# One operation for scale and modulation in the norms, query tokens first, modulation chunks moved, retention's gain folded into its gate

## What is computed

```python
def first_block(...):                      # DEPTH = 2
    for l in range(2):
        # six vectors of 1024 each, from c and from c_ctx: shift, scale, gate (mix), shift, scale, gate (ffn)
        sh_a, sc_a, g_a, sh_f, sc_f, g_f = adaln(c, mod_w[l], mod_b[l])
        csh_a, ... = adaln(c_ctx, mod_w[l], mod_b[l])
        hx = modulate(rms_norm(x, norm_mix_g[l]), sh_a, sc_a)      # n(x) * (1 + scale) + shift
        hc = modulate(rms_norm(ctx, norm_mix_g[l]), csh_a, csc_a)
        y_x, y_c = even_mixer(...) if l == 0 else odd_mixer(...)   # odd: queries from hx alone, keys and values from both
        x = x + g_a * (y_x @ w_out[l])
        x = x + g_f * swiglu(modulate(rms_norm(x, norm_ffn_g[l]), sh_f, sc_f), ...)
        # the same for ctx in layer 0

def second_block(...):                     # DEPTH = 2
    ...
    hr = retention_chunkwise(...)                                   # 4 heads of 512
    y_r = silu(rg) * (normalized(hr) * r_norm_g[i])                 # gate, norm, weight
    merged = sigmoid(gm) * (y_m @ w_bm[i]) + sigmoid(gr) * (y_r @ w_br[i])
    ...
    x = x + sigmoid(h3 @ w_pe_gate[i]) * (p[i] @ w_pe[i])
    return rmsnorm(x, final_g)
```

## Time and profile before

| | before |
|---|---|
| median of 3 runs | 2436.9 us (2436.57 to 2437.91) |
| profiled execution: time, span | 2438.51 us, 2436.7 us |
| busy: TensorE, VectorE, ScalarE | 95%, 62%, 42% of the span |
| mean granted clock of TensorE | 0.979 of full speed |
| chain that ended last | TensorE 83%, VectorE 9%, ScalarE 3%, waits without a cause in the profile 2%, DMA 2% |
| HBM read | 386 MB, 159 GB/s over the span |

### The profile page before, as it was taken

The page is one execution under the profiler, slowest core; times in us unless marked ns, Lnnn a source line. Parts: engine busy times, 40 slices in busy tenths (PEclk is TensorE's granted clock), DMA queues, the critical chain, the costliest instruction groups (busy, mean ns, idle before and its releaser), DMA issues.

```text
span 2436.7 us, 33036 instructions
## 1 busy us (share of the span) xinstructions
PE 2307.2 (95%) x14198; PEld 1987.7 (82%) x14198; DVE 1513.5 (62%) x1866; ACT 1015.4 (42%) x1223; POOL 0.2 (0%) x4
## 2 busy tenths in 40 slices
PE   6978989999998888999999999999999999999997
PEld 3755667777786767999999877999989988789997
DVE  3877553333347667555678767675668766767475
ACT  4245541111224145434664345443456534444343
POOL 0000000000000000000000000000000000000000
PEclk9989999999998999999999999999999999999999
DMA  8440034444323241455555453555445445344552
GB/s 321 169 176 1 25 139 192 166 188 170 124 104 121 87 104 64 146 189 190 212 199 183 175 186 138 182 177 187 182 182 203 178 177 194 143 173 178 186 183 94
DMA packets 61401, 389.19 MB, mean 160 GB/s; under 512 B 6600, under 2 KB 11080, under 8 KB 16072
## 3 DMA queue, kind: packets, MB, share of 16 engines
q1 hardware_dynamic: 61256, 387.08, 43.6%
HBM read 386.01 MB, written 1.05 MB: 159 GB/s over the span
## 4 chain that ended last, share of the span: by engine, by line
PE 83%; DVE 9%; ACT 3%; issue 2%; DMA 2%; SPq 0%; DVEq 0%; ACTq 0%
PE PS L479 25%; PE PS L480 25%; PE PS L481 25%; DVE w_lo L1565 2%; DMA raw<-chunks_in 1%; PE PS L783 1%; PE PS L929 1%; PE PS L665 1%; ACT w_hi L1135 1%; PE PS L626 1%; DVE stat L1760 1%; PE PS L911 1%; PE PS L690 1%; ACT xn L1213 1%; DVE BIG L1769 1%
## 5 line engine op out<-in xcount | busy, mean ns | idle before, releaser
L1565 DVE TENSOR_TENSOR w_lo<-raw,w_hi 128x2048 fp32r<-128x2048 f32 x300 | 683.5, 2290 | 506.7 <-ACT w_hi L1135 504.9
L1135 ACT ACTIVATE w_hi<-raw 128x2048 fp32r<-128x2048 f32 x300 | 571.7, 1913 | 749.5 <-PE PS L481 448.8
L479 PE MATMUL PS<-x_hi,w_hi 128*128 128x256 f32 (+1 forms) x2048 | 629.4, 307 | 12.2 <-DVE x_lo L1630 7.8
L480 PE MATMUL PS<-x_lo,w_hi 128*128 128x256 f32 (+1 forms) x2048 | 626.9, 306 | 0.0
L481 PE MATMUL PS<-x_hi,w_lo 128*128 128x256 f32 (+1 forms) x2048 | 626.5, 306 | 0.0
L479 PEld LDWEIGHTS PS<-x_hi,w_hi 128*128 128x128 f32 x2048 | 393.9, 192 | 38.0 <-issue 21.1
L480 PEld LDWEIGHTS PS<-x_lo,w_hi 128*128 128x128 f32 x2048 | 394.0, 192 | 16.7
L481 PEld LDWEIGHTS PS<-x_hi,w_lo 128*128 128x128 f32 x2048 | 393.8, 192 | 16.8
L479 PE MATMUL PS<-w_hi,x_hi 128*128 128x512 f32 (+1 forms) x800 | 317.7, 397 | 21.6 <-DVE w_lo L1565 9.8
L480 PE MATMUL PS<-w_lo,x_hi 128*128 128x512 f32 (+1 forms) x800 | 313.6, 392 | 0.0
L481 PE MATMUL PS<-w_hi,x_lo 128*128 128x512 f32 (+1 forms) x800 | 313.2, 391 | 0.0
(11 more groups left out here) (284 smaller groups left out, 2259.5 us busy)
## 6 DMA issues: line engine op xcount, KB each, us to landing
raw<-chunks_in SPq DMA_DIRECT2D x348, 1024.0 KB, 4.8
bias_ring<-brows_in SPq DMA_DIRECT2D x32, 256.0 KB, 5.1
G<-nrows_in SPq DMA_DIRECT2D x2, 1536.0 KB, 6.6
free_b<-rel_in SPq DMA_DIRECT2D x4, 512.0 KB, 8.0
BIG<-rel_in SPq DMA_DIRECT2D x4, 512.0 KB, 9.1
tabt<-tabs_in SPq DMA_DIRECT2D x1, 1536.0 KB, 12.3
X<-x_in SPq DMA_DIRECT2D x1, 1024.0 KB, 8.3
X<-ctx_in SPq DMA_DIRECT2D x1, 1024.0 KB, 10.3
```

The source lines that it names most:

```text
L479: pe.matmul(o, lhs[0], rhs[0], start=start, stop=False, **more)
L480: pe.matmul(o, lhs[0], rhs[1], start=False, stop=False, **more)
L1135: act.activation(w_hi[:, i % HI_RING, :], ring[:, n % RING, :], ACT.Copy).then_inc(*hi_ready.now(n))
L1565: dve.tensor_tensor(w_lo[:, c % RING, :], ring[:, c % RING, :], w_hi[:, i % HI_RING, :].bitcast(F32), ALU.subtract).then_inc(*lo_ready.now(c))
```

## The change

- **Norms.** Outside ("mix", 0) VectorE makes scale and modulation in one operation: X times the modulation's scale times the broadcast root, 256 columns each; ScalarE adds the shift while it rounds to `x_hi`; VectorE's subtraction adds the shift as well. In ("mix", 0) the 8 products with the root come first, each linked to the next by a wait; then the modulation's values, the `w_lo` of the first weight chunk, and then for each tile scale and shift on VectorE from SBUF, with the rounding on ScalarE.
- **Query tokens first.** In ("mix", 1) all 8 tiles of the query tokens come before the 8 of the context tokens, since the first product (`od_q`) takes query tokens alone; the `w_hi` and `w_lo` of its third and fourth chunk go between the context tiles.
- **Modulation chunks.** In `w_out` of layer 0 two mod chunks stand after its first, second and fourth chunk (6 in place of 4). Pack 3 is turned after the third chunk, its copy and its values (`modulation(3)`, `modulation(0, 2)`) move ahead of squares and into the residual. The SwiGLU holds 2 mod chunks fewer; `mod_end(1, 0)` moves to before its last product. `ffn_step` stays as it is. At the start the fifth mod chunk goes between the two halves of `root_of_squares`.
- **`w_lo` out of the residuals.** One `w_lo` each moves from within the residuals of `w_out` and of the last `ffn_out` of layer 0 to behind them.
- **Retention.** The weight is multiplied into the gate `rg` (`gained`, four operations of 2 x 512 columns) while the heads are still computed; its four operations in `norm_r` go.
- **The end.** The table load of the square root stands after the third pair of squares, and VectorE's sums of the third pair after its last addition to X.

```diff
+        def who_order(key, tiles):
+
+            return [(0,), (1,)] if key == ("mix", 1) else [tuple(range(tiles // 2))]
...
-            def root_of_squares(key, tiles, bank=7):
+            def root_of_squares(key, tiles, bank=7, meanwhile=None):
 
                 acc, n = sums[tiles][0], tiles * P
                 pe.wait_ge(*x_summed.after(key, KD - 1))
@@ -591,9 +595,11 @@
                 for t in range(tiles):
                     mm = pe.matmul(PS[:, bank, t:t + 1], acc[:, t * P:(t + 1) * P], tab("ones")[:, 0:1], start=True, stop=True)
                 mm.then_inc(*sums_bc.now(key))
+                if meanwhile:
+                    meanwhile()
                 pe.wait_ge(*rstd_diag.after(key))
                 pe.matmul(PS[:, bank, 0:n], tab("ones"), sums[tiles][2][0], start=True, stop=True).then_inc(*rstd_bc.now(key))
-                reader[bank] = scaled.after(key, KD - 1)
+                reader[bank] = scaled.after(key, tiles // 2 - 1, KD - 1)
...
+            def mod_two():
+
+                mod_chunk()
+                mod_chunk()
...
+                    if l == 0 and last:
+                        mod_end(1, 0)
...
-                    if l == 0 and part == 1:
-                        mod_end(1, 0)
...
-            project_feat("w_out", 0, 2, hT[4], width=512, freed=updated("w_out", 0), need=copied("y0"), between=mod_row)
-            mod_end(0, 2)
+            project_feat("w_out", 0, 2, hT[4], width=512, freed=updated("w_out", 0), need=copied("y0"),
+                         between=at_steps({0: mod_two, 1: mod_two, 2: lambda: mod_end(0, 2), 3: mod_two}))
...
+                for whos in who_order(key, tiles):
+                    for k in range(KD):
+                        act.wait_ge(*scaled.after(key, whos[-1], k))
+                        for w in whos:
+                            cols = slice(w * 256, w * 256 + 256)
+                            if key != ("mix", 0):
+                                ins = act.activation(hT[tiles][0][:, k, cols], full[tiles][:, k, cols], ACT.Identity,
+                                                     bias=modc[l][:, kind * 8 + k, w:w + 1])
+                        if key == ("mix", 0):
+                            ins = act.activation(hT[tiles][0][:, k, :], full[tiles][:, k, :], ACT.Copy)
+                        ins.then_inc(*copied_s.now(key, whos[-1], k))
+                        if middle and k + KD * whos[0] in middle:
+                            middle[k + KD * whos[0]]()
...
             split_to(first + 2)
+            modulation(3)
             for k in range(KD):
                 act.wait_ge(*x_ready.after("w_out", 0, k // 4, k % 4))
                 square(("ffn", 0), 4, k)
                 if k == 3:
                     split_to(first + 3)
                     split_to(first + 4)
-            modulation(3)
...
+            first_od = place_of[plan["first chunk", "od_q", 1]]
+            norm_mod(("mix", 1), 4, 0, {8: lambda: split_to(first_od + 2), 12: lambda: split_to(first_od + 3)})
...
-                    if l and n == 3:
-                        act.activation(stat[:, 20:21], eps, ACT.Sqrt)
                     for m in (n - 1, n) if n % 2 else ():
                         act.wait_ge(*x_ready.after("pe_g", l, m // 2, m % 2))
                         for k in (2 * m, 2 * m + 1):
                             tail(key, k, l == 0)
+                        if l and m == 2:
+                            act.activation(stat[:, 20:21], eps, ACT.Sqrt)
...
+                early = key == ("mix", 0)
+
+                def scale(whos, k):
+                    for w in whos:
+                        cols = slice(w * 256, w * 256 + 256)
+                        o = full[tiles][:, k, cols]
+                        if early:
+                            ins = dve.tensor_scalar(o, o, modc[l][:, kind * 8 + 8 + k, w:w + 1],
+                                                    modc[l][:, kind * 8 + k, w:w + 1], ALU.mult, ALU.add)
+                            continue
+                        ins = dve.scalar_tensor_tensor(full[tiles][:, k, cols], X[:, w, k, :],
+                                                       modc[l][:, kind * 8 + 8 + k, w:w + 1], PS[:, bank, cols], ALU.mult, ALU.mult)
+                    ins.then_inc(*scaled.now(key, whos[-1], k))
+
+                def low(whos, k):
+                    dve.wait_ge(*copied_s.after(key, whos[-1], k))
+                    if early:
+                        hi, lo = (a[:, k, :] for a in hT[tiles])
+                        ins = dve.tensor_tensor(lo, full[tiles][:, k, :], hi.bitcast(F32), ALU.subtract)
+                    for w in () if early else whos:
+                        cols = slice(w * 256, w * 256 + 256)
+                        hi, lo = (a[:, k, cols] for a in hT[tiles])
+                        ins = dve.scalar_tensor_tensor(lo, full[tiles][:, k, cols], modc[l][:, kind * 8 + k, w:w + 1],
+                                                       hi.bitcast(F32), ALU.add, ALU.subtract)
+                    ins.then_inc(*copied_v.now(key, k if whos[-1] == tiles // 2 - 1 else ("x", k)))
+
+                if early:
+                    for k in range(KD):
+                        link(dve.tensor_tensor(full[tiles][:, k, :].rearrange("p (w t) -> p w t", w=2), X[:, :, k, :],
+                                               PS[:, bank, 0:n].rearrange("p (w t) -> p w t", w=2), ALU.mult))
                     modulation(*mod)
-                for k in range(KD):
-                    if k + lead < KD:
-                        scale(k + lead)
-                    low(k)
+                if ahead:
+                    ahead()
+                steps = [(whos, k) for whos in who_order(key, tiles) for k in range(KD)]
+                for step in steps[:lead]:
+                    scale(*step)
+                for i, step in enumerate(steps):
+                    if i + lead < len(steps):
+                        scale(*steps[i + lead])
+                    low(*step)
                     if at_tile:
-                        at_tile(k)
+                        at_tile(i)
...
+                        first_od = place_of[plan["first chunk", "od_q", 1]]
+                        residual("ffn_out", l, 5, 2 * part, key, lambda j, i: lo_to(first_od - 2 + 2 * j) if i == 0 else None)
+                        lo_to(first_od + 1)
...
+            def ahead(j, i):
+                if i == 0:
+                    lo_to(ev + 12 + j)
+                if (j, i) == (1, 0):
+                    modulation(0, 2)
+
+            residual("w_out", 0, 2, 0, ("ffn", 0), ahead)
+            lo_to(ev + 14)
+            norm_mod(("ffn", 0), 4, 2, None, lambda k: lo_to(ev + 15) if k == 5 else None)
             swiglu(0, 4, ("mix", 1))
-            norm_mod(("mix", 1), 4, 2, None, lambda k: lo_for("ffn_out", 0, 5) if k == 3 else None)
+            first_od = place_of[plan["first chunk", "od_q", 1]]
+            norm_mod(("mix", 1), 4, 2, None, lambda i: lo_to(first_od + 2 + (i > 9)) if i in (9, 13) else None)
...
-                    for t in range(2):
-                        ins = dve.tensor_tensor(hr[t][:, cols], hr[t][:, cols], G[:, 1024:3072][:, cols], ALU.mult)
-                    link(ins)
                     for t in range(2):
                         ins = dve.tensor_tensor(hr[t][:, cols], hr[t][:, cols], rg[:, t, cols], ALU.mult)
                     link(ins, y_ready, "yr", l, part)
                     if part == 0:
                         merge_m(l, 0)
                         lo_to(first_bm + 3)
+
+            def gained(l, j):
+
+                dve.wait_ge(*tok_acted.after("rg", l, j, 0))
+                cols = slice(512 * j, 512 * j + 512)
+                gain = G[:, 1024:3072][:, cols].unsqueeze(1).to_broadcast([P, 2, 512])
+                link(dve.tensor_tensor(rg[:, :, cols], rg[:, :, cols], gain, ALU.mult))
...
                         if h == 3:
                             lo_for("gr", l, 1)
+                            gained(l, 2)
                             copy_turned(("ym", l), 0, 4)
                         biased("gr", l, 1, wide(gr), h - 2)
+                    if h < 2:
+                        gained(l, h)
                     if h in (1, 2):
                         r_out(h - 1)
                 r_copy(2)
+                gained(l, 3)
                 copy_turned(("ym", l), 4, 4)
                 head_stats("hr", 2, hr, 512)
...
-                    if n % 2:
+                    if n == 1 or n == 3 and l == 0:
                         finish(key, [k - 2, k - 1], l == 0)
                     dve.wait_ge(*tok_acted.after("pe_g", l, n))
                     link(dve.tensor_tensor(t, t, pw[:, k:k + 2, :], ALU.mult))
                     dve.tensor_tensor(X[:, 0, k:k + 2, :], t, X[:, 0, k:k + 2, :],
                                       ALU.add).then_inc(*x_ready.now("pe_g", l, n // 2, n % 2))
+                    if n == 3 and l:
+                        finish(key, [k - 2, k - 1], False)
```

(6 more changed lines are left out.)

55 lines of the change are left out of this document (13 added, 42 removed).

## The result

| | before | after |
|---|---|---|
| median (7 runs each, side by side) | 2437.22 us | 2445.96 us |
| range | 2436.57 to 2439.76 | 2442.55 to 2447.87 |
| profiled execution: time, span | 2438.51, 2436.7 us | 2447.41, 2445.6 us |
| mean granted clock | 0.979 | 0.975 |

The change makes the kernel slower: ratio 1.0031 (95% interval 1.0022 to 1.0040), some 8.7 us by the medians (7.6 by the ratio) in place of the forecast gain of 6.1. In the code after, the products of a weight chunk are L483 to L485 (L479 to L481 before), mod chunks L789 (L783), turns of modulation rows L768 (L762), turns of activations L632 (L626), `w_hi` L1146, `w_lo` L1574, ScalarE's copy of a pack L1297.

What follows compares the result with a forecast made beforehand. The prediction took TensorE to bound the kernel (83% of the chain). Its terms, +11.6 for new SwiGLU waits less slot 11, then -2.1, -1.4, -6.3, -0.7, -5.2, -2.05, summed to -6.15: median 2430.8 us, range 2423 to 2438.

Steps and rivals of the forecast that it cites:

- The start: First product of `ev_in`: earlier load, then three scale steps and one subtraction (2.7 us), starting at 38.45; -2.1 us.
- Two moves in `w_out` I cost at nothing.: In `w_out`: pack 3's copy ahead of the squares, and two mod chunks between weight chunks in SyncE's load queue; no cost.
- The third is released by a mod chunk and has a whole weight chunk of time to arrive, as before.: In `w_out`: the third weight chunk's load, with the changed order, still arrives in time; no cost.
- The rival "slower": SwiGLU: loads behind the two copies take longer in a full transfer queue; from 10.4 us on, +5, 2442 us; chance 0.06.
- The two new waits at slots 3 and 7: SwiGLU, layer 0: TensorE's turn waits for ScalarE's copies in slots 4 and 8; 7.3 us each plus 2.6 of clock.
- Slot 11: SwiGLU, layer 0: pack 6 is complete after slot 10, so the 5.61 us wait goes, with 2.6 of clock.
- Norms: First product follows the broadcast by 3.3, 1.85 and 1.85 us; ("ffn", 0) -1.4, ("mix", 1) -6.3, ("ffn", 1) -0.7.
- the second wait and the half clock behind ("mix", 1): Behind norm ("mix", 1): the 1.31 us wait at 759.99 goes, and the restart at half clock shortens, -0.5.
- The fifth mod chunk: At the start: running it before the broadcast brings the load waiting for it forward; counted as 1.75 us (0 to 3.4).
- Retention: Two operations fewer in each part close TensorE's holes of 0.86 and 1.74 us; -2.6 per layer, -5.2 in both.
- "No new waits": SwiGLU: rows of packs 4 and 5 are ready in time, so no holes at slots 3 and 7; 2411 us; chance 0.10.
- "Two narrow operations cost more than one wide": Norms: each new 256-wide VectorE operation takes 0.48 us, not 0.41; sum -4.3, 2432.6 us; chance 0.05.

Runs made afterwards that it cites:

- e1: The changed kernel with the bank's release at the start of ("mix", 0) signalled by the last product with the root, its last reader; 2440.46 us, ratio 1.0002.
- e6: The changed kernel with bank release corrected, pack copies one slot earlier, and `w_out`'s second weight chunk loaded and used right behind the first; 2416.93 us, ratio 0.9910.
- e2: The changed kernel with `w_hi` and `w_lo` of `w_out`'s second weight chunk moved behind the attention's first turned copies; 2440.27 us, ratio 1.0005.
- e10: The kernel before with only the SwiGLU's last turn (`mod_end`) in layer 0 moved ahead of its last product, no chunk moved; 2431.43 us, ratio 0.9973.
- e3: The changed kernel with ScalarE's copies of packs 4, 5 and 6 in SwiGLU slots 3, 7 and 11, not 4, 8 and 12; 2423.73 us, ratio 0.9936.
- e7: The changed kernel with bank release corrected and mod chunks of `w_out` and SwiGLU back where they were, late last turn kept; 2411.36 us, ratio 0.9888.
- e9: As e7, with the fifth mod chunk at the start behind the broadcast again, not between the halves of `root_of_squares`; 2415.00 us, ratio 0.9909.
- e8: The kernel before with only the change's retention part (weight multiplied into the gate) and its end part; 2430.19 us, ratio 0.9972.

## Why the prediction was wrong

**The sign.** Of the terms that it had, all but the start came out within about 1 us. Three waits that it lacked (for a bank at the start, for a load ahead of the attention, for a load in `w_out`), with the clock behind them, cost 15 us. The first broke a term of the sum, the second had no term at all, the third had been put at nothing.

1. *The start* (forecast -2.1, measured +3.8). The working gave the first product at 38.45. With the bank's release mended it comes at 38.70 (e1): each duration in it held, the load included (`w_hi` forecast between 31.35 and 33.25, measured 31.78). What failed is "three scale steps and one subtraction", which follows only what the product reads. A product also waits for the bank that it writes. In the code before, `reader[bank] = scaled.after(key, KD - 1)` named the product with the root, the last reader of the bank that holds the broadcast. After, the same name is signalled by an operation from SBUF to SBUF that ends at 44.3 us, where the last read of PSUM ends at 30.5 (24.75 + 5.74). The diff shows this line, and the prediction quotes it nowhere. Cost: 5.7 us, shown by e1.
2. *"Two moves in `w_out` I cost at nothing."* The order of chunks was traced from `w_out` onwards, and not backwards: the same order decides when the second weight chunk can be loaded ahead of the attention, where `split_to(first_ev + 11)` counts weight chunks alone. The prediction named SyncE's queue, but followed it only forward from `w_out`, not to the loads released before the attention. Cost: 4.5 us at the turn, and 3.6 in the attention behind it. e2 and e6 show that it was the order of loads: e2 gives some 6 us of it back, and with e6's order both the wait (7.49) and the attention (100.5) are as before.
3. *"The third is released by a mod chunk and has a whole weight chunk of time to arrive, as before."* It was released by a mod chunk, and had 12.9 us until TensorE was ready for it (304.94 to 317.88). But "as before" was a misreading: before, the first weight chunk released it, with no other load beside it. Now three loads of 1 MB came at once, the transfer took 9.35 us in place of some 4.8 (that in slot 3 of this trace, 447.70 to 452.46, took 4.76), and the two splits behind it take 4 more. The rival "slower" had just this mechanism, longer loads in a full queue, and looked for it at the two copies in the SwiGLU. Cost: 1.6 us (e6: gone).

The Trainium skill, "DMA: Bandwidth & Descriptors", section "Issuing engines are not separate DMA queues", says that DMAs "will ultimately run on the same 16 DMA engines and interleave with each other", whichever engine started them. Here all come from SyncE, and the trace agrees: the last of three loads in flight together took twice as long as one alone.

**The terms that held.** The two new waits at slots 3 and 7: 7.36 and 7.27 us (forecast 7.3), with the clock 19.8 forecast, 20.9 by e3. The prediction's bounds for one restart, 1.7 to 3.4 us, come from none of its rows; the runs show 2.7 (e10: 8.3 less the wait of 5.61) and 3.1 (e3: 20.9 less the two waits, halved), around its 2.6. Slot 11: -8.2 forecast, -8.3 by e10's trace; but the reason given was wrong in part. It put the end of this wait down to a pack that is complete one slot earlier; e10 and e7 show that the later turn does it without. Norms: TensorE idle for 1.85, 1.85 and ("ffn", 0) 3.42 us ahead of the first product, forecast 1.85, 1.85 and 3.3. What was over-sized is the second wait and the half clock behind ("mix", 1): 1.8 us were forecast for the two together, and some 0.75 came.

```profile
352.41 0.76 PE L483 MATMUL PS<-x_hi,w_hi 128*128 128x512 f32 x1 [3.42 <-DVE x_lo L1654]
...
769.41 0.77 PE L483 MATMUL PS<-w_hi,x_hi 128*128 128x512 f32 x1 [1.85 <-DVE x_lo L1654]
...
997.70 0.55 PE L483 MATMUL PS<-x_hi,w_hi 128*128 128x256 f32 x1 [1.85 <-DVE x_lo L1654]
```

The fifth mod chunk: 1.75 forecast, 1.5 by e9. Retention: 2.6 per layer forecast, 2.6 of idle time and 3.0 by the shift in e8. The end: -2.05 forecast, and the wait ahead of the last sum fell from 7.09 to 4.94:

```profile
2436.30 1.22 PE L582 MATMUL PS<-G,tabt 128*128 128x256 f32 x2 [4.94 <-DVE G L1609]
```

**The rivals.** "No new waits" fell by the two rows of the SwiGLU. "Two narrow operations cost more than one wide" fell too: three of them in a row took 1.26 us, 0.42 each, the forecast's 0.41:

```profile
767.60 1.26 DVE L1642 SCALAR_TENSOR_TENSOR xn<-X,bias_ring,PS 128x256 f32<-128x256 f32 x3 [2.17 <-PE PS L601]
```

The Trainium skill, "VectorE: DVE Perf Modes", section on the TRN2 errata, warns of a fixed latency per operation and advises 512 elements. A single one does show 0.47 us (median of the 40 at L1642), but in a row the next begins before that has passed, and ahead of the first product of the norm ("ffn", 0) the split into two cost 0.1 us at most (3.42 against 3.3).

**The range** of 2423 to 2438 was made from the bounds of the known terms and had no room for a wait that was not listed. The chance of 0.08 for "slower" rested on one rival (0.06) and on the tail of the same sum.

**What stays open.** The longer wait alone does not set what the attention costs behind it. Over the 22 us from the turn on, and up to the turn of y0 (columns as above), in this order: after (wait 12.47 us; 104.4 us to y0), e3 (12.49; 104.2), e1 (12.47; 101.9) and before (7.43; 100.8):

```profile
183.20:205.20 22.00, 18.22 (x85) 13.33 (x86) 12.62 (x29) 9.51 (x26) 0.00 (x0) 0.72 0.00 1
```
```profile
183.06:205.06 22.00, 18.23 (x87) 13.39 (x88) 12.82 (x28) 9.72 (x27) 0.00 (x0) 0.73 0.00 1
```
```profile
178.10:200.10 22.00, 17.59 (x96) 12.35 (x96) 14.87 (x33) 11.68 (x32) 0.00 (x0) 0.86 0.00 1
```
```profile
174.90:196.90 22.00, 17.39 (x102) 12.66 (x104) 15.84 (x36) 11.87 (x33) 0.00 (x0) 0.91 0.00 1
```

The same instructions behind the same wait ran at a mean granted clock of 0.72, 0.73 and 0.86. So of the 3.6 us that the attention lost, 1.1 are there in e1 as well, and nothing recorded separates the rest further.

## What to carry to other kernels

When the operation behind a semaphore's name changes, list everyone who waits for that name: an event that frees a buffer has to be signalled by the buffer's last reader, and moving work off PSUM moves the release with it unless it is renamed. When the order of loads changes in a ring, follow it backwards too: wherever an engine splits a chunk ahead of its use, ask which chunk now releases that load and how many loads are released with it. And try a large reordering against its smallest part: here two moved lines (e10) gave the one gain that came with moving the chunks.

## What was not expected of the hardware

Of three loads of 1 MB released within 2 us, the last landed 9.35 us after its release; one alone landed after 4.7 to 4.8, the second of a burst after 6.21. And the cost of a wait in granted clock is not a constant of the wait: after 12.5 us idle the next 22 us had a mean clock of 0.72, 0.73 and 0.86 in three kernels' executions, with the same work. A wait of 1.31 us left the clock full, one of 2.54 at the same place was followed by 15 us at a mean of 0.89.
